# Sliding-window heads of a two-block transformer kernel: values stationary in column strips, the divided probabilities moving, the output written turned

## The reference

```
scores = q . k / 8, for keys at a distance of 0 to 127 behind the query; else masked
m      = max(max over keys of scores, sink[h])
p      = exp(scores - m)
den    = sum over keys of p + exp(sink[h] - m)
out    = (p / den) @ v                     # 256 x 64 for each of 16 heads
y      = out of all heads (256 x 1024) @ w_up_sw
```

## Time and profile before

| | us |
|---|---|
| median of 3 runs | 1720.12 (1720.10 to 1720.28) |
| the profiled execution | 1719.93 |
| its span, first to last instruction | 1718.1 |

### The profile page before, as it was taken

The page is one execution under the profiler, slowest core; times in us unless marked ns, Lnnn a source line. Parts: engine busy times, 40 slices in busy tenths (PEclk is TensorE's granted clock), DMA queues, the critical chain, the costliest instruction groups (busy, mean ns, idle before and its releaser), DMA issues.

```text
span 1718.1 us, 28196 instructions
## 1 busy us (share of the span) xinstructions
PE 1699.7 (99%) x10757; PEld 1402.4 (82%) x10757; DVE 1171.6 (68%) x2216; ACT 916.8 (53%) x1666; POOL 236.0 (14%) x350
## 2 busy tenths in 40 slices
PE   9999999999999999999999999999999999999998
PEld 8888878888888878888787878888888787878887
DVE  6656667766566776768877775556678877766665
ACT  5355475453553753656645455555666545464553
POOL 2200300022012000243203000000333203000000
PEclk9999999999999999999999999999999999999999
DMA  8443544555444445643323455554633333455552
GB/s 312 158 169 123 172 130 164 177 195 179 152 132 159 139 148 173 217 139 123 124 94 106 148 171 173 195 196 151 235 114 115 124 100 112 159 172 188 182 181 87
DMA packets 137120, 270.09 MB, mean 157 GB/s; under 512 B 5535, under 2 KB 8731, under 8 KB 136987
## 3 DMA queue, kind: packets, MB, share of 16 engines
q1 hardware_dynamic: 134928, 265.44, 46.1%
q10 hardware_dynamic: 2059, 2.85, 0.5%
HBM read 267.23 MB, written 1.05 MB: 156 GB/s over the span
## 4 chain that ended last, share of the span: by engine, by line
PE 92%; DVE 3%; ACT 3%; issue 2%; POOL 1%; DVEq 0%; POOLq 0%; ACTq 0%
PE bank L421 23%; PE bank L423 22%; PE bank L422 22%; PE bank L402 5%; PE bank L450 3%; PE bank L404 3%; PE bank L1687 1%; DVE lo L384 1%; PE bank L1664 1%; PE bank L613 1%; PE bank L1591 1%; PE bank L1630 1%; PE bank L1599 0%; ACT hi L374 0%; PE bank L411 0%
## 5 line engine op out<-in xcount | busy, mean ns | idle before, releaser
L421 PE MATMUL bank<-hi,xhl 128*128 128x512 f32 (+1 forms) x1792 | 724.3, 404 | 3.0 <-DVE lo L384 2.1
L423 PE MATMUL bank<-hi,xhl 128*128 128x512 f32 (+1 forms) x1792 | 698.3, 390 | 0.0
L422 PE MATMUL bank<-lo,xhl 128*128 128x512 f32 (+1 forms) x1792 | 695.8, 388 | 0.0
L384 DVE TENSOR_TENSOR lo<-raw,hi 128x1024 fp32r<-128x1024 f32 (+1 forms) x504 | 611.4, 1231 | 48.3 <-PE bank L423 37.2
L374 ACT ACTIVATE hi<-raw 128x1024 fp32r<-128x1024 f32 (+1 forms) x504 | 519.7, 1051 | 231.2 <-PE bank L423 209.9
L421 PEld LDWEIGHTS bank<-hi,xhl 128*128 128x128 f32 x1792 | 337.0, 188 | 77.8 <-issue 14.7
L423 PEld LDWEIGHTS bank<-hi,xhl 128*128 128x128 f32 x1792 | 336.3, 188 | 72.9
L422 PEld LDWEIGHTS bank<-lo,xhl 128*128 128x128 f32 x1792 | 337.6, 188 | 59.7
L402 PE MATMUL bank<-xhl,hi 128*128 128x512 f32 x384 | 136.0, 398 | 0.0
L404 PE MATMUL bank<-xhl,lo 128*128 128x256 f32 x384 | 107.8, 281 | 0.0
L402 PEld LDWEIGHTS bank<-xhl,hi 128*128 128x128 f32 x384 | 72.2, 188 | 17.8
(11 more groups left out here) (316 smaller groups left out, 1887.5 us busy)
## 6 DMA issues: line engine op xcount, KB each, us to landing
raw<-in_w_in SPq DMA_DIRECT2D x135, 1024.0 KB, 5.1
raw<-in_w_ff SPq DMA_DIRECT2D x64, 1024.0 KB, 5.3
raw<-in_w_proj_a SPq DMA_DIRECT2D x8, 1024.0 KB, 5.1
raw<-in_w_proj_b SPq DMA_DIRECT2D x8, 1024.0 KB, 5.0
raw<-in_w_out SPq DMA_DIRECT2D x8, 1024.0 KB, 5.1
raw<-in_w_up_sw SPq DMA_DIRECT2D x8, 1024.0 KB, 4.9
raw<-in_w_up_dn SPq DMA_DIRECT2D x8, 1024.0 KB, 5.0
raw<-in_w_o SPq DMA_DIRECT2D x8, 1024.0 KB, 5.2
```

The costliest lines, as they stand in the source:

```text
L384: dve.tensor_tensor(self.lo[g % LO_RING][:, 0:w], src, self.hi[g % HI_RING][:, 0:w].bitcast(F32), ALU.subtract).then_inc(self.lo_ready, 1)
L421: pe.matmul(out, xh[:, row, t], self.hi[slot % HI_RING][:, w], start=first, stop=False)
L422: pe.matmul(out, xh[:, row, t], self.lo[slot % LO_RING][:, w], start=False, stop=False)
L423: mm = pe.matmul(out, xl[:, row, t], self.hi[slot % HI_RING][:, w], start=False, stop=last)
```

## The change

In words:

- The reciprocal is applied earlier: a new step `s_norm` scales the probabilities in place on ACT (two instructions), before the transpose.
- `s_out` works on two heads at once. The values are stationary (128 keys x 64 features), one head in the column strip of partitions 0 to 63, the other in 64 to 127; the turned probabilities move, 256 columns for the first key block and 128 for the second. The output arrives with features on partitions, so it is the cut operand already: ACT copies it to `xh[1]`, DVE writes `xl[1]`. The four turns of `ys` and their cuts are gone.
- A new list `turned_values` of 19 groups: the turn of head t-2, the scaling of head t-1, the scores of head t, and in even groups from 4 on the output of the pair t/2-2. The last two groups (turn of 15; output of pair 7) go into delta slots 0 and 1.
- `prob` and `masked` become one ring of four tiles, worked in place; `turned` becomes a ring of three.
- The first `rows` and `betas` steps take banks 4, 5, 6 and 7 in place of 6, 4, 7 and 5.

```diff
--- before.py
+++ after.py
@@ -206,6 +206,17 @@
...
                    + ([(f"{kind}_out", t - 2)] if t >= 2 else []))
+    return out
+
+
+def turned_values(kind, heads):
+
+    out = []
+    for t in range(heads + 3):
+        out.append(([(f"{kind}_turn", t - 2)] if 2 <= t <= heads + 1 else [])
+                   + ([(f"{kind}_norm", t - 1)] if 1 <= t <= heads else [])
+                   + ([(f"{kind}_scores", t)] if t < heads else [])
+                   + ([(f"{kind}_out", t // 2 - 2)] if t >= 4 and t % 2 == 0 else []))
     return out
@@ -1100,7 +1111,7 @@
...
 
-    work = [[w for kind in ("s_turn", "s_scores", "s_out") for w in group if w[0] == kind] for group in attention("s", HEADS)]
+    work = turned_values("s", HEADS)
     p.run(sec("dk", D), [[("rope", "sk", 0), ("rope", "sk", 1), ("rope", "sq", 0)], [("rope", "sq", 1)], [], [],
@@ -1110,7 +1121,7 @@
...
 
-    slots = delta_slots(work[17])
+    slots = delta_slots(work[17:])
     p.run(sec("gb", at_sw + small + 2 * CH + D), slots[:16], halves=True)
@@ -1150,7 +1161,8 @@
...
 
-    put(0, *last)
+    for at, steps in enumerate(last):
+        put(at, *steps)
     for at, kind in ((0, "rows"), (2, "betas"), (2, "decays"), (4, "gram"), (8, "unit")):
@@ -1175,9 +1187,8 @@
...
     put(21, ("silu", "dv"))
-    for at, name, n in ((1, "dv", 0), (9, "dv", 1), (11, "dv", 2), (17, "dv", 3), (21, "kd", 0), (27, "ys", 0),
-                        (25, "v", 0), (29, "ys", 1), (26, "v", 1), (29, "v", 2), (31, "v", 3), (42, "ys", 2),
-                        (43, "ys", 3), (45, "kd", 1), (55, "yd", 0), (57, "yd", 1), (61, "yd", 2)):
+    for at, name, n in ((1, "dv", 0), (9, "dv", 1), (11, "dv", 2), (17, "dv", 3), (21, "kd", 0), (25, "v", 0),
+                        (26, "v", 1), (29, "v", 2), (31, "v", 3), (45, "kd", 1), (55, "yd", 0), (57, "yd", 1), (61, "yd", 2)):
         put(at, ("turn", name, n))
...
@@ -1201,7 +1211,7 @@
...
 
-    early = {("rows", 2): SCORE[0], ("betas", 2): TURN, ("rows", 3): SCORE[1], ("betas", 3): OUT,
+    early = {("rows", 0): SCORE[0], ("rows", 1): SCORE[1], ("betas", 0): TURN, ("betas", 1): OUT, ("rows", 2): SCORE[0], ("betas", 2): TURN, ("rows", 3): SCORE[1], ("betas", 3): OUT,
              ("gram", 3): SCORE[1], ("gram_q", 0): 3, ("gram_q", 1): 3, ("gram_q", 2): 2, ("gram_q", 3): 3}
@@ -1337,19 +1347,17 @@
...
     k_dec = flat8[:, 0:1024].rearrange("p (h d) -> p h d", d=P)
-    source = {"sq": b0, "sk": k_dup, "dq": b0, "dk": b1, "dv": b1, "ys": ys, "yd": vb,
-              "mix": qs}
-    xt_of = {"ys": 1, "yd": 0, "mix": 1}
-    half_of = {"ys": 1.0, "mix": 0.5}
+    source = {"sq": b0, "sk": k_dup, "dq": b0, "dk": b1, "dv": b1, "yd": vb, "mix": qs}
+    xt_of = {"yd": 0, "mix": 1}
+    half_of = {"mix": 0.5}
     tap = lambda j, n: 2 * KB + 1 + j * 3 * DHEADS + n
...
     wide_tile = 3 * P + TB
-    prob = [scr[:, i * wide_tile:(i + 1) * wide_tile] for i in range(2)]
-    masked = [scr[:, (2 + i) * wide_tile:(3 + i) * wide_tile] for i in range(2)]
+    prob = [scr[:, i * wide_tile:(i + 1) * wide_tile] for i in range(4)]
     sink_column = (P, 3 * P + 1)
     with_sink = [(0, slice(0, P + 1)), (1, slice(P + 1, wide_tile))]
-    turned = [scr[:, 2304 + i * 384:2304 + (i + 1) * 384] for i in range(2)]
+    turned = [scr[:, 1544 + i * 384:1544 + (i + 1) * 384] for i in range(3)]
     junk = scr[:, 3072:4096]
...
@@ -1585,22 +1593,26 @@
...
                     core.free(pe, TURN)
-                    pe.wait_ge(*at("s_prob", h))
+                    pe.wait_ge(*at("s_scaled", h))
                     for c in range(3):
                         first = c * P + (c > 0)
-                        mm = pe.transpose(B[TURN][:, c * P:c * P + P], prob[h % 2][:, first:first + P], core.ident)
+                        mm = pe.transpose(B[TURN][:, c * P:c * P + P], prob[h % 4][:, first:first + P], core.ident)
                     mm.then_inc(*up("s_turned", h))
...
                 if kind == "s_out":
-                    h = arg
+
                     core.free(pe, OUT)
-                    pe.wait_ge(*at("s_copied", h))
-                    v = slice(HD * (h // (HEADS // 2)), HD * (h // (HEADS // 2)) + HD)
-                    pe.matmul(B[OUT][:, 0:HD], turned[h % 2][:, 0:P], vs[:, 0, v], start=True, stop=True)
-                    pe.matmul(B[OUT][:, HD:2 * HD], turned[h % 2][:, P:2 * P], vs[:, 0, v], start=True, stop=False)
-                    pe.matmul(B[OUT][:, HD:2 * HD], turned[h % 2][:, 2 * P:3 * P], vs[:, 1, v],
-                              start=False, stop=True).then_inc(*up("s_summed", h))
-                    core.hold(s, OUT, "ys", h)
+                    pe.wait_ge(*at("s_copied", 2 * arg + 1))
+                    strips = [(slice(HD * m, HD * m + HD), turned[(2 * arg + m) % 3]) for m in range(2)]
+                    k = 2 * arg // (HEADS // 2)
+                    v = slice(HD * k, HD * k + HD)
+                    for r, p in strips:
+                        pe.matmul(B[OUT][r, 0:S], vs[:, 0, v], p[:, 0:2 * P], start=True, stop=False, skip_group_check=True)
+                    for r, p in strips:
+                        mm = pe.matmul(B[OUT][r, P:S], vs[:, 1, v], p[:, 2 * P:3 * P], start=False, stop=True,
+                                       skip_group_check=True)
+                    mm.then_inc(*up("s_summed", arg))
+                    core.hold(s, OUT, "cut", ("ys", arg))
                 b = delta_bank(kind, arg) if kind in DELTA_BANK else None
@@ -1888,20 +1900,29 @@
...
                     act.wait_ge(*at("s_max", h))
-                    if h >= 2:
-                        act.wait_ge(*at("s_turned", h - 2))
                     act.wait_ge(*at("s_sink", h))
                     for tb, cols in with_sink:
-                        ins_ = act.activation(prob[h % 2][:, cols], masked[h % 2][:, cols], ACT.Exp, scale=-1.0,
+                        ins_ = act.activation(prob[h % 4][:, cols], prob[h % 4][:, cols], ACT.Exp, scale=-1.0,
                                               bias=t1.negmax[:, h % 2, tb:tb + 1],
...
                     act.wait_ge(*at("s_turned", h))
-                    if h >= 2:
-                        act.wait_ge(*at("s_summed", h - 2))
-                    act.activation(turned[h % 2], B[TURN][:, 0:3 * P], ACT.Copy).then_inc(*up("s_copied", h))
+                    if h >= 3:
+                        act.wait_ge(*at("s_summed", (h - 3) // 2))
+                    act.activation(turned[h % 3], B[TURN][:, 0:3 * P], ACT.Copy).then_inc(*up("s_copied", h))
+                if kind == "s_norm":
+
+                    h = arg
+                    act.wait_ge(*at("s_inverse", h))
+                    for tb, first in ((0, 0), (1, P + 1)):
+                        part = prob[h % 4][:, first:first + (tb + 1) * P]
+                        ins_ = act.activation(part, part, ACT.Copy, scale=t1.inverse[:, h % 4, tb:tb + 1])
+                    ins_.then_inc(*up("s_scaled", h))
+                if kind == "s_out":
+                    act.wait_ge(*at("s_summed", arg))
+                    act.activation(core.xh[1][:, arg, :], B[OUT][:, 0:S], ACT.Copy).then_inc(*up("high", ("ys", arg)))
                 if kind == "decays":
@@ -2181,20 +2202,17 @@
...
                     h = arg
-                    negative_max(dve, core, s, B[SCORE[h % 2]], masked[h % 2], t1.negmax[:, h % 2, :], parts, 2,
-                                 ("s_scored", h), ("s_prob", h - 2) if h >= 2 else None, ("s_max", h),
+                    negative_max(dve, core, s, B[SCORE[h % 2]], prob[h % 4], t1.negmax[:, h % 2, :], parts, 2,
+                                 ("s_scored", h), ("s_turned", h - 4) if h >= 4 else None, ("s_max", h),
                                  t.negsink_all[:, layer, h:h + 1], apart=1)
-                if kind == "s_turn":
+                if kind == "s_norm":
                     h = arg
...
                 if kind == "s_out":
-                    h = arg
-                    dve.wait_ge(*at("s_summed", h))
-                    dve.wait_ge(*at("s_inverse", h))
-                    dve.tensor_tensor(ys[:, :, h * HD:h * HD + HD],
-                                      B[OUT][:, 0:2 * HD].rearrange("p (t d) -> p t d", t=TB),
-                                      bcast(t1.inverse[:, h % 4, :], 2, HD), ALU.mult).then_inc(*up("ys", h))
+                    dve.wait_ge(*at("high", ("ys", arg)))
+                    dve.tensor_tensor(core.xl[1][:, arg, :], B[OUT][:, 0:S], core.xh[1][:, arg, :].bitcast(F32),
+                                      ALU.subtract).then_inc(*up("cut", ("ys", arg)))
                 if kind == "rows":
@@ -2316,10 +2334,10 @@
...
                     h = arg
-                    if h >= 2:
-                        pool.wait_ge(*at("s_prob", h - 2))
+                    if h >= 4:
+                        pool.wait_ge(*at("s_turned", h - 4))
                     for column in sink_column:
```

(2 more changed lines are left out.)

4 lines of the change are left out of this document (2 added, 2 removed), and 1 row of the table TURN_BANK.

## The result

The changed kernel takes 1730.34 us (median of 4 runs, 1729.53 to 1731.49) against 1720.12 of the kernel before: ratio 1.0059, 95% interval 1.0047 to 1.0072. It is slower by 10.2 us; the forecast was 1719.6, with a range that ended at 1725. The profiled execution took 1731.49 us, span 1729.7.

The account below looks back on a forecast made before the run. PE, busy 99% of the span, was taken as the bound until another queue ends later. Profiled 1719.93 + 3.0 (stages longer) - 3.5 (`ys` turns) = 1719.4, given as 1719.6 us against the median; range 1710 to 1725.

Parts of the forecast that it names:

- PE's saving: Whole kernel, if PE never waits: 8.2 us from the strips plus 3.5 from the `ys` turns, 11.7 us.
- the loop VectorE, ScalarE, VectorE: Even slots: subtract waits for ScalarE's copy, behind exp, behind VectorE's max; 9.17 us a round against PE's 8.44.
- The strips: Output matmuls of two heads in two 64-column strips side by side: 0.80 us a pair instead of 1.31.
- The `ys` turns: Delta stage: four turns a layer removed, 0.41 us each; 3.3 us on PE, taken as 3.5 in all.
- The loop's sum: From one even slot's max to the next, by distances between starts: 9.17 us, against 8.95 before.
- Low halves and recip behind taps 1.34: VectorE's step behind a convolution turn's taps: 1.34 us of the loop, read from the trace of before.
- rival B: Slots: GpSimd's late sink column delays exp and lengthens all loops, 2.3 us more a layer: 1724.2 us; chance 0.13.
- The stand at the squares: Slot 12: PE waits 3.2 us for the TURN bank ahead of the sum of squares, which starts at 799.5.
- the last turn: Turn 15: PE waits 1.8 us by way of root, sink column, exp and scaling.
- A: Whole kernel: nothing waits and PE's whole saving comes through, 1708.4 us; chance 0.20.
- C: Output strips don't run side by side: 1.5 us instead of 0.8, 0.7 a layer, 1721.0 us; chance 0.10.
- The chance of slower: Whole kernel above 1723.6 us: 0.20, against 0.26 for faster and 0.54 for same.

Follow-up runs that it names:

- output first: Changed kernel with ScalarE's copy and VectorE's subtraction of a finished pair queued ahead of that slot's scaling, maximum and exponential: 1718.02 us, ratio 0.9986.
- product cut short: Changed kernel with GpSimd's second silu product for the keys covering 8 of each 256 columns: 1722.89 us, ratio 1.0014.
- both waits filled: Kernel with GpSimd's product cut to 8 of 256 columns, plus idle matmuls: twelve ahead of the sum of squares, seven ahead of the last turn: 1721.11 us.
- waits mostly removed: Changed kernel with pair's copy and subtraction at the slot's very head, sum of squares a slot later in the outputs' bank, root a slot later: 1713.09 us.
- tanh a slot later: Changed kernel with the keys' tanh steps (ScalarE's tanh and GpSimd's two silu products) one slot later: 1729.02 us, ratio 1.0054.
- that with the `ys` turns: Kernel with the pair's output first in the queues (1718.0 us), with the four removed `ys` turns put back on PE, unread: 1721.01 us.
- strips in another order: The 1713.1 us version with a pair's four strip matmuls issued first strip twice, then second strip twice: 1712.64 us, ratio 0.9956.

## Why the prediction was wrong

- **What bounds.** Right: PE's saving counts only until another queue ends later, and the loop VectorE, ScalarE, VectorE is what ended later. With its wait taken out (output first) the kernel gained 12.3 us, the clock's part among them.
- **PE's saving.** The strips, 0.80 us, right. The `ys` turns were taken at 3.5 us; between and rest gave back 1.2 + 1.5 = 2.7, and 2.4 by the same windows, 3.0 by the medians, came back as cost when they were put in again. Too high by 0.8 in the profiled execution, by 0.4 to 1.1 in the other kernels.
- **The loop's sum: the step that failed.** "Low halves and recip behind taps 1.34" was a row of before, taken as the price of the operation. It measured 2.19, and the sum 10.00 instead of 9.17. The row already held a meeting, and the rows of before showed it: the same operation stands there at 1.35 and 1.34 us behind taps and at 1.21 beside them. GpSimd's product in before:

```profile
761.47 1.27 POOL L2335 TENSOR_TENSOR buf<-buf,scratch 128x512 f32<-128x512 f32 x1
```

It ends at 762.74, 0.26 us after the low half's start; the low half took 0.14 more than 1.21. In after the product has 1.11 us to go (770.73 to 771.84), and the low half takes 0.97 more. With the output first, the low half has 0.72 to go when the product starts (769.72 to 770.44), and the product takes 0.59 more. In all three the later one is longer by what the earlier one had left, less 0.12 to 0.14. The meeting got longer because the taps came forward: before, they stood behind the multiply and PE's turn and started 2.02 us after the maximum (765.90 to 767.92), and now 0.67 (766.56 to 767.23), while the product stayed behind ScalarE's exp and tanh. The Trainium skill (SBUF — State Buffer, "SBUF: two separate sides") has a rule for it: a VectorE operation with two SBUF inputs and a GpSimd operation share ports under an exclusive lock, the first to start holds it for its whole instruction and the other is blocked. For the low half and the product these traces agree with it; for GpSimd's instruction ahead of the product they do so where the low half came first (2.33 us for 1.50), and not where GpSimd did: with 0.42 us left it did not lengthen the low half. The prediction priced this meeting for the sink column (rival B) and not for the low half. Cost: slots of 97.2 us against 93.6 without product and without a fall of the clock, 3.6 a layer, 7.2 in all.
- **The waits.** The stand at the squares (2.88 for 3.2) and at the last turn (1.74 for 1.8) came as laid out in length, though not in time: the squares start at 802.66, not at 799.5, since PE and the copy it waits for are both late by the longer loops. With the failed term out (product cut short, no fall of the clock in layer one) the slots took 1.3 us more than before, where 1.5 was forecast. But a stand was priced at its own length alone. The granted clock fell to 0.50 behind it, which cost 2.8 and 1.5 us in the profiled execution, some 3 by the medians. This was nowhere in the sum, nor among the rivals.
- **The sum again**, for the profiled execution: 1719.4 + 7.2 (low half) + 4.3 (clock) + 0.8 (turns) - 0.4 (the slots' 1.3 for 1.5, two layers) = 1731.3, measured 1731.49. All but the first term are differences of the table's columns, so that the sum meets the time is no test. The test was the kernel with the product cut short and both waits filled: 1721.11 us, where 1719.6 or a little less was expected.
- **The rivals.** A did not happen: with the waits mostly removed, 1713.1 is what came of its 1708.4. B is real and acts in after once a layer, in the first round (0.58 us); in the later ones the exp follows its own maximum. It acts again as soon as the product is moved. C is out by the 0.80 and by the starts in pairs (last section). The chance of slower, 0.20, was too low, because both missing terms come from waits and meetings, and here both added.

## What to carry to other kernels

A duration read beside another engine's work is the operation plus the meeting: before it goes into the sum of a loop, look up who ran beside it, and work out whether the change makes them meet for longer. When a result goes from PE over two engines, put its copy ahead of the steps that wait for the next item (here that edit was worth 12.3 us, the clock's fall that went with it included); and price a new stand of PE not at its length alone but with the slow matmuls that may stand behind it, or move the step to where its bank is free.

## What the runs showed of the hardware

- VectorE's two-operand low half and GpSimd's product exclude each other, whichever starts first: 1.22 against 2.19 us for the one, 1.29 against 1.88 for the other. GpSimd's one-input instruction ahead of the product took 2.33 us instead of 1.50 when it started inside a low half (784.13, tanh a slot later), but when it came first the low half kept its 1.22.
- The clock's fall is not certain at a given stand. In the kernel with the product cut short PE stood 2.88 us in layer one and 2.87 in layer two; behind the first the granted clock stayed at 1.00 and the squares took 1.07 us, behind the second it was 0.54 and they took 1.94. At the last turn a stand of 1.95 us brought it to 0.50 in one profile, and one of 1.95 in another did not. Of the kernels with 11 runs, the three with stands of 1.4 us and more (product cut short, output first, and that with the `ys` turns) spread over 3.1 to 3.7 us, the three without over 0.9 to 1.3.

```profile
799.02 1.07 PE L1566 MATMUL bank<-buf,square 128*32 128x512 f32 x8 [2.88 <-ACT scratch L1914]
```

```profile
1309.50:1312.00 2.50, 2.21 (x9) 0.55 (x10) 0.68 (x4) 2.28 (x9) 0.00 (x0) 0.54 0.00 0
```

- Matmuls into two column strips run side by side. In the trace of the strips in another order the eight instructions start in pairs no more than 0.02 us apart (761.36, 761.63, 761.84, 761.95), and a pair of heads takes 0.81 us to the next piece; issued in turns it took 0.80. Which of a pair belongs to which strip the trace doesn't say.
